# One decoder step: rankings and pairs of the third token tile spread over its u and v rows, element sums gathered 14 rows ahead in pieces of 8, and two final norms moved among the tail's rows

## The chip, the core and the metric

The program runs on one core of a Trainium2 chip. The metric is the device time of one execution in microseconds (us). Four compute engines matter: TensorE (PE in the rows), VectorE (DVE), ScalarE (ACT) and GpSimd (POOL); SyncE (SP) issues loads. All transfers go through the core's 16 DMA engines. Everything is float32.

## What is computed

One layer of a hybrid decoder for 512 prompt tokens and 32 sample tokens: three gated branches (a recurrent block, latent attention, cross-attention) are merged and added to x, then comes PEER, a lookup of experts, and a last RMSNorm. The change touches PEER and what follows it:

```python
q = einsum('td,dhpk->thpk', hb, w_peer_query)              # 8 heads, 2 halves, 128
s = einsum('thpk,hpnk->thpn', q, peer_sub_keys)            # 128 scores per half
s1, i1 = top_k(s[:, :, 0], 16); s2, i2 = top_k(s[:, :, 1], 16)
cand = s1[..., :, None] + s2[..., None, :]                 # 16 x 16 pairs per head
top, sel = top_k(cand, 16); idx = the 16 pairs' expert numbers
w = softmax(top)
act = gelu(einsum('thkd,td->thk', peer_u[idx], hb))
out = einsum('thk,thkd->td', w * act, peer_v[idx])         # 128 rows of 2048 per token
y = rmsnorm(x + out, g_final)
```

## The kernel before

Tokens are cut into tiles of 128: tile 3, tile 4 (the 32 samples), and tiles 0, 1, 2. Each token picks 8 x 16 = 128 experts. One "row" of the kernel is one indirect gather of 128 x 2048 floats, which brings expert number r for each of the tile's 128 tokens: 1,048,576 bytes. `JOBS` is the order of rows: u and v of tile 3, u and v of tile 4 (32 rows each, since the samples are folded four to a partition group), u of tile 2, then v of tiles 2, 0 and 1. GpSimd issues every row (L615) into a ring of five buffers (six in the v rows from tile 2 on). It issues a row only when VectorE has used the row that held the buffer before (`rows_used`). VectorE uses a u row by a multiply with a sum (L2072) and a v row by a multiply-add (L2097 for the samples, L2275 into PSUM for tiles 2, 0, 1).

Tiles 0 and 1 (`DENSE`) have no u rows. In their stead TensorE multiplies their activations with all 16,384 experts (L1217, 128 loads of 1 MiB, the "dense" stage), ScalarE copies each block of 512 columns out (L1566) and stores it to a DRAM tensor `products`. When all are stored, GpSimd gathers the needed sums from it one element per token at a time (L645, the "element gathers", 256 of them), and VectorE turns them into weights a piece of `CHUNK` at a time: `chunk_in` waits for the piece and does the first half of the gelu, ScalarE does the tanh, `chunk_out` the rest. GpSimd holds the element gathers back until v row `HELD` of tile 2, where it waits for the last stored product. From there each v row is followed by one element gather, or by two until it is `AHEAD` rows ahead.

The order on VectorE is written out by hand. `take(n)` uses the next n rows, `upto(r)` uses rows up to a given one. In the stage before the dense one, the "query stage", TensorE makes 16 query blocks (L1196) and scores them; per block u VectorE ranks tile 2's scores (`rank_b`, six instructions, L1987 to L2195) and then takes rows. TensorE may run two blocks ahead of the ranking. `pairs_b(t, h0)` makes the candidate pairs of two heads, ranks them and writes their expert numbers; GpSimd waits for these numbers (`idx_ready`) before rows that need them. `rank_kept` ranks four of the 32 stored score blocks of tiles 0 and 1. The queues on each engine are in order, so whatever waits holds what is written behind it. The final norm of a tile is `square` on ScalarE, `norm_scale` on VectorE, a root on ScalarE, `norm_rows` on VectorE, and a store by SyncE in the order of `FINAL`.

## Time and profile before

| | before |
|---|---|
| median of 3 runs | 4435.69 us (4435.52 to 4441.54) |
| profiled execution, span | 4435.2 us (its own time is not listed apart; the lowest listed run is 0.3 us above the span, the median 0.5 us) |
| PE busy | 3608.9 us (81%) |
| DVE busy | 2800.4 us (63%) |
| ACT busy | 387.1 us (9%) |
| POOL busy | 1465.4 us (33%) |
| moved by DMA | 1409.18 MB, 318 GB/s over the span |

Shares over the whole span mix stages with different limits. The last query block ends before 2785.69 us, the dense stage runs from there to 3660.65 us, and what follows to 4435.2 us is v rows with no TensorE work to speak of (here "the tail"). A megabyte of these rows is 10^6 bytes, so that one gathered row counts 1.0486 MB.

### The profile page before, as it was taken

What the parts mean: (1) busy time and instruction counts of PE and PEld (TensorE: products, weight loads), DVE (VectorE), ACT (ScalarE), POOL (GpSimd) and SP (SyncE); (2) the same over time, 40 slices, a digit from 0 to 9 for tenths busy, and PEclk for the clock granted to TensorE, in tenths of its full rate; (3) what the DMA queues carried; (4) which work ended last, traced back from release to release, by engine and by line L of the source; (5) the groups of instructions that cost most, each with busy time, mean ns of one, the idle gap of its engine ahead of it and who ended that gap; (6) DMA issues with size and microseconds to landing.
All of it is one profiled execution on the core that took longest, in us unless ns stands there. A gap on an engine that the chain in (4) does not pass through costs nothing.

```text
span 4435.2 us, 37982 instructions
## 1 busy us (share of the span) xinstructions
PE 3608.9 (81%) x13874; PEld 2263.2 (51%) x13874; DVE 2800.4 (63%) x3704; ACT 387.1 (9%) x897; POOL 1465.4 (33%) x1217
## 2 busy tenths in 40 slices
PE   9999999998999999999999999999999990000000
PEld 7888856645998575555555456444444440000000
DVE  5233324431000378887887668888885558999998
ACT  1012123321000100000000010000000001000000
POOL 0000100042000035454455444333322226777772
PEclk9999999999999999999999999999999995555555
DMA  4211361158666599999999989999999999999998
GB/s 183 76 68 67 118 222 43 43 185 293 244 240 247 207 390 399 412 418 400 384 406 421 418 358 370 412 405 417 419 401 423 423 423 374 395 409 410 410 410 368
DMA packets 224180, 1409.18 MB, mean 318 GB/s; under 512 B 33312, under 2 KB 44448, under 8 KB 60000
## 3 DMA queue, kind: packets, MB, share of 16 engines
q0 software_dynamic: 135632, 899.39, 50.0%
q1 hardware_dynamic: 75072, 471.89, 27.7%
q10 hardware_dynamic: 13296, 35.52, 2.1%
q8 instruction: 110, 1.80, 0.2%
q14 instruction: 70, 0.57, 0.0%
HBM read 1380.91 MB, written 25.75 MB: 317 GB/s over the span
## 4 chain that ended last, share of the span: by engine, by line
PE 69%; DMA 12%; DVE 6%; POOL 6%; issue 6%; ACT 1%; SPq 0%; DVEq 0%; POOLq 0%; ACTq 0%
PE psum L1217 20%; PE psum L1076 17%; PE psum L670 13%; DMA arena<-in_v,arena 10%; POOL arena L615 4%; PE psum L1196 4%; PE psum L1181 3%; POOL arena L645 2%; DVE arena L2111 2%; DVE psum L2275 2%; PE psum L1144 2%; PE psum L1124 1%; PE psum L743 1%; PE psum L753 1%; PE psum L904 1%
## 5 line engine op out<-in xcount | busy, mean ns | idle before, releaser
L1076 PE MATMUL psum<-arena 128*128 128x160 f32 (+1 forms) x5120 | 1174.1, 393 | 2.6 <-DMA arena<-in_w_merge 1.8
L2275 DVE SCALAR_TENSOR_TENSOR psum<-arena,psum 128x2048 f32<-128x2048 f32 x381 | 897.1, 2355 | 215.4 <-DMA arena<-in_v,arena 207.9
L1076 PEld LDWEIGHTS psum<-arena 128*128 128x128 f32 x5120 | 834.2, 190 | 342.1 <-DMA arena<-in_w_merge 2.0
L615 POOL DMA_INDIRECT arena<-in_v,arena x544 | 638.9, 1174 | 783.3 <-DVE psum L2275 365.0
L1217 PE MATMUL psum<-arena 128*128 128x512 f32 x2048 | 879.2, 592 | 0.6 <-ACT arena L1559 0.6
L615 POOL DMA_INDIRECT arena<-in_u,arena x288 | 462.2, 1605 | 1131.7 <-DVE arena L2028 504.0
L1217 PEld LDWEIGHTS psum<-arena 128*128 128x128 f32 x2048 | 389.1, 190 | 490.1 <-issue 490.1
L670 PE MATMUL psum<-arena 128*128 128x272 f32 x2432 | 565.0, 394 | 8.7 <-DMA arena<-in_w_proj 8.7
L670 PEld LDWEIGHTS psum<-arena 128*128 128x128 f32 x2432 | 461.9, 191 | 108.8 <-issue 14.8
L2072 DVE CUSTOM_DVE_ANT_1 arena<-arena 128x2048 f32<-128x2048 f32 x160 | 361.7, 2289 | 59.6 <-DMA arena<-in_u,arena 58.8
L2111 DVE SCALAR_TENSOR_TENSOR arena<-arena,pages 128x2048 f32<-128x2048 f32 x128 | 300.9, 2351 | 87.6 <-DMA arena<-in_v,arena 83.7
L2072 DVE CUSTOM_DVE_ANT_0 arena<-arena 128x2048 f32<-128x2048 f32 x128 | 288.5, 2289 | 20.1 <-DMA arena<-in_u,arena 18.1
L645 POOL DMA_INDIRECT arena<-products,arena x256 | 247.3, 966 | 94.1 <-issue 79.8
L562 POOL DMA_INDIRECT arena<-in_pool_keys,pages x48 | 45.9, 955 | 434.4 <-PE psum L885 415.3
L1196 PE MATMUL psum<-arena 128*128 128x384 f32 x512 | 167.7, 486 | 1.3 <-ACT arena L1491 1.3
L1181 PE MATMUL psum<-arena 128*128 128x512 f32 x384 | 167.7, 596 | 0.0
L1652 DVE TENSOR_TENSOR arena<-psum,arena 128x544 f32<-128x544 f32 x31 | 22.4, 724 | 219.3 <-PE psum L670 217.6
L550 POOL TENSOR_TENSOR arena<-arena 128x544 f32<-128x544 f32 x16 | 21.7, 1396 | 359.2 <-PE psum L670 359.2
L1471 ACT ACTIVATE arena<-psum 128x160 f32<-128x160 f32 (+1 forms) x96 | 38.1, 397 | 1125.7 <-PE psum L1076 1105.6
L1196 PEld LDWEIGHTS psum<-arena 128*128 128x128 f32 x512 | 96.2, 190 | 65.4 <-ACT arena L1491 1.6
L1181 PEld LDWEIGHTS psum<-arena 128*128 128x128 f32 x384 | 72.8, 192 | 88.1 <-issue 87.9
L1929 DVE SCALAR_TENSOR_TENSOR arena<-arena,psum 128x160 f32<-128x160 f32 (+1 forms) x32 | 14.0, 436 | 164.4 <-PE psum L1076 164.1
(312 smaller groups left out, 2559.4 us busy)
## 6 DMA issues: line engine op xcount, KB each, us to landing
arena<-in_w_merge SPq DMA_DIRECT2D x160, 1024.0 KB, 6.7
arena<-in_u_cols SPq DMA_DIRECT2D x128, 1024.0 KB, 9.5
arena<-in_w_out SPq DMA_DIRECT2D x32, 1024.0 KB, 6.3
arena<-in_w_query SPq DMA_DIRECT2D x32, 1024.0 KB, 6.9
arena<-in_w_proj SPq DMA_DIRECT2D x31, 1024.0 KB, 4.9
products<-arena ACTq DMA_DIRECT2D x32, 512.0 KB, 13.8
arena<-in_pool_keys SPq DMA_DIRECT2D x80, 160.0 KB
arena<-in_v,arena POOLq DMA_INDIRECT x544, 12.0
```

The source lines that it names most:

```text
L562: pool.indirect_dma_start(key_slots[2 * n % KSLOTS][:, j, :], None, A["pool_keys"], bass.IndirectOffsetOnAxis(ap=page_rows[:, pg:pg + 1], ...
L615: pool.indirect_dma_start(row, None, A[table], bass.IndirectOffsetOnAxis(ap=idx[:, r:r + 1], axis=0))\
L645: pool.indirect_dma_start(dense_acts[:, e:e + 1], None, products, bass.IndirectOffsetOnAxis(ap=elem_idx[:, e // P, e % P:e % P + 1], axis=0))\
L670: last = mm(out[:, a, :], w, rhs[:, a * HALF:(a + 1) * HALF], start=start, stop=stop)
L1076: last = mm(out, w[:, (off + k) * P:(off + k + 1) * P], src[:, k0 + k, lo:hi], start=(k == 0), stop=(k == n - 1))
L1144: last = mm(psum[:, 5 + u % 2, 0:A_N], w[:, k * P:(k + 1) * P], hfT_a[:, k, :], start=(k == 0), stop=(k == KD - 1))
L1181: last = mm(psum[:, 3 * (n % 2) + t, :], merged_b[:, 4 * q + k, t * P:(t + 1) * P], w[:, k, :], start=(q == 0 and k == 0), stop=(q == 3 an ...
L1196: last = mm(psum[:, u % 2, 0:B_N], w[:, k * P:(k + 1) * P], hfT_b[:, k, :], start=(k == 0), stop=(k == KD - 1))
L1217: last = mm(psum[:, 4 + DENSE * (b % 2) + t, :], hfT_b[:, k0 + k, t * P:(t + 1) * P], w[:, k, :], start=(k0 + k == 0), stop=(k0 + k == KD ...
L2072: V.tensor_tensor_reduce(row, row, h, 1.0, 0.0, ALU.mult, ALU.add, out).then_inc(s("rows_used"), 1)
L2111: V.scalar_tensor_tensor(lone, row, atmp_3[:, r:r + 1], lone, ALU.mult, ALU.add).then_inc(s("rows_used"), 1)
L2275: V.scalar_tensor_tensor(a, four(row), atmp_b[:, t, r:r + 1], a if r else four(x1_b[:, t, :]), ALU.mult, ALU.add).then_inc(s("rows_used"), 1)
```

## The change

- In the query stage, VectorE takes no rows at u = 0 to 3 and at u = 8, two at u = 9, three at the others (before: three at each but u = 3). The pairs of heads 0 and 1 of tile 2 are made one head at a time, at u = 1 and u = 3; those of heads 2 and 3 at u = 8.
- After it, the first stored ranking comes at u row 36 of tile 2 (before: at the 31st), the groups of four follow at distances of 5 and 6 rows (before 4 or so), the pairs of tile 0 behind u rows 99 to 117, and all four pairs of tile 1 go among the v rows of tile 2 (before: one of them).
- `HELD` goes from 100 to 116, `AHEAD` from 36 to 14, `CHUNK` from 32 to 8; the element gathers count on three semaphores in turn instead of two.
- The final norms of tile 3 and of the samples move from v rows 116 to 123 of tile 2 to v rows 12 to 43 of tile 0. Tile 2's norm now comes first in `FINAL`. The samples' sum uses PSUM banks 0 to 3 once tile 2's norm has read them.
- Three one-use semaphores become one (`lam_ready`).

```diff
-FINAL = (3, 4, 2, 0, 1)
-HELD = 100
-AHEAD = 36
-CHUNK = 32
+FINAL = (2, 3, 4, 0, 1)
+HELD = 116
+AHEAD = 14
+CHUNK = 8
+ELEMS = 3
@@ def idx_count(t, r)
-    return 4 * PAIRS.index(t) + r // 32 + 1
+    split = t < 2 or (t == 2 and r >= 16)
+    return 4 * PAIRS.index(t) + r // 32 + 1 + split
@@ GpSimd
-                    if table == "u" and t != 4 and r % 32 == 0:
+                    if table == "u" and t != 4 and (r % 32 == 0 or (t, r) == (2, 16)):
-                                .then_inc(s(f"elems_landed{e // CHUNK % 2}"), 16)
+                                .then_inc(s(f"elems_landed{e // CHUNK % ELEMS}"), 16)
@@ TensorE
             pe.wait_ge(s("x1_done"), 2)
+            pe.wait_ge(s("y_done"), 1)
             for n in range(4):
-                last = mm(psum[0:SAMP, 4 + n, :], gather4, ...)
+                last = mm(psum[0:SAMP, n, :], gather4, ...)
@@ ScalarE, behind the last product
-            act.wait_ge(s("x1_done"), 1)
-            square("fin", 3, spare, lone)
-            norm_root("fin", 3, 0)
-            act.wait_ge(s("x1_sample"), 1)
-            square("fin", 4, spare[0:SAMP], x1_s[0:SAMP])
-            norm_root("fin", 4, 1)
-            for turn, t, chunks in ((2, 2, (0,)), (3, 0, (1, 2, 3, 4)), (4, 1, (5, 6, 7))):
-                for k in chunks:
-                    gelu_chunk(k)
-                act.wait_ge(s("x1_done"), turn + 1)
-                square("fin", t, four(spare), acc[turn % 2])
-                norm_root("fin", t, turn)
+            per = P // CHUNK
+            gelu_chunks(0, 1)
+            act.wait_ge(s("x1_done"), 3)
+            square("fin", 2, four(spare), acc[0])
+            norm_root("fin", 2, 0)
+            gelu_chunks(1, 2)
+            act.wait_ge(s("x1_done"), 1)
+            square("fin", 3, spare, lone)
+            norm_root("fin", 3, 1)
+            gelu_chunks(2, 4)
+            act.wait_ge(s("x1_sample"), 1)
+            square("fin", 4, spare[0:SAMP], x1_s[0:SAMP])
+            gelu_chunks(4, 5)
+            norm_root("fin", 4, 2)
+            gelu_chunks(5, per + 1)
...
@@ VectorE, pairs of nh heads instead of two
-            def pairs(t, h0, v16, i16, cand, eq, small, rows_between):
+            def pairs(t, h0, v16, i16, cand, eq, small, rows_between, nh=2):
@@ VectorE, query stage, for u in range(16)
-                if u == 3:
-                    pairs_b(2, 0)
-                take(0 if u == 3 else 3)
+                if u in (1, 3):
+                    pairs_b(2, u // 2, 0, 1)
+                if u == 8:
+                    pairs_b(2, 2)
+                take(0 if u < 4 or u == 8 else 2 if u == 9 else 3)
@@ VectorE, u rows of tile 2
-            upto(1)
-            pairs_b(2, 2)
             for n in range(4):
-                upto(7 + 4 * n)
+                upto(36 + 5 * n)
                 rank_kept(4 * n)
-            upto(24)
+            upto(56)
             pairs_b(2, 4)
             for n in range(4):
-                upto((31, 35, 40, 44)[n])
+                upto(63 + 6 * n)
                 rank_kept(16 + 4 * n)
...
+            for n in range(4):
+                upto(99 + 6 * n)
+                pairs_b(0, 2 * n)
+            upto(122)
             share_tops(w_b[:, 2:3, :], tsum_b[:, 2 * PH:3 * PH], 2, s("w_b_ready"))
-            pairs_b(1, 4)
-            upto(P - early - 1)
+            upto(P)
@@ VectorE, v rows
-                        if r == 5:
-                            pairs_b(1, 6, 0)
-                        if r == 10:
+                        if r in (4, 11, 18, 25):
+                            pairs_b(1, 2 * (r // 7), 0)
+                        if r == 32:
                             shift_tops(w_b[:, 0:2, :], tsum_b[:, 0:2 * PH], (0, 1))
...
-                        if r == 116:
-                            norm_scale("fin", 3, 0)
+                    if job == 1:
+                        if r == 12:
+                            norm_scale("fin", 3, 1)
+                        if r == 18:
+                            norm_rows("fin", 3, 1, lone, lone, gain_f, "y_done")
...
+                        if r == 43:
+                            norm_rows("fin", 4, 2, x1_s[0:SAMP], x1_s[0:SAMP], gain_f[0:SAMP], "y_done")
```

The first place is VectorE in the query stage. Before, each ranking of a block (six instructions that begin with MAX) is followed by three v rows of the samples (L2097); here stand the end of one ranking, its rows, and the ranking behind them.

```order
L1993 MAX arena<-arena 128x8
L1995 MAX_INDEX arena<-arena 128x8
L2195 CAST arena<-arena 128x16
L2097 SCALAR_TENSOR_TENSOR arena<-arena,newmask 128x2048 x3
L1987 MAX arena<-psum 128x8
```

After, between the same ranking (its CAST is now L2214) and the next one there is no row; rows stand again only behind u = 4. These are the rankings of u = 2 and u = 3 and the beginning of one head's pairs (L2031):

```order
L2214 CAST arena<-arena 128x16
L2005 MAX arena<-psum 128x8
L2007 MAX_INDEX arena<-arena,psum 128x8
L2009 MATCH_REPLACE arena<-arena,psum 128x128
L2011 MAX arena<-arena 128x8
L2013 MAX_INDEX arena<-arena 128x8
L2214 CAST arena<-arena 128x16
L2031 TENSOR_TENSOR arena<-arena 128x256
```

In all, 47 rows stand in the query stage before (three at 15 of the blocks, two inside the pairs), and 34 now. The other 13 stand behind it, where 26 rows now follow one another before the first stored ranking.

The second place is GpSimd where the element gathers (`products`) begin among the v rows. Before, they begin behind 101 rows:

```order
L615 DMA arena<-in_u,arena 128x2048 x128
L615 DMA arena<-in_v,arena 128x2048 x101
L645 DMA arena<-products,arena 128x1
L615 DMA arena<-in_v,arena 128x2048
L645 DMA arena<-products,arena 128x1
```

After, behind 117 rows, and the double ones are two instead of eight; the second fence is the place where they stand.

```order
L622 DMA arena<-in_u,arena 128x2048 x128
L622 DMA arena<-in_v,arena 128x2048 x117
L652 DMA arena<-products,arena 128x1
L622 DMA arena<-in_v,arena 128x2048
L652 DMA arena<-products,arena 128x1
```

```order
L652 DMA arena<-products,arena 128x1
L622 DMA arena<-in_v,arena 128x2048
L652 DMA arena<-products,arena 128x1 x2
L622 DMA arena<-in_v,arena 128x2048
L652 DMA arena<-products,arena 128x1 x2
L622 DMA arena<-in_v,arena 128x2048
L652 DMA arena<-products,arena 128x1
```

The number of element gathers is 256 in both; the rows that follow the last one are 36 before and 14 now.

The third place is VectorE among the v rows of tile 0 in the changed kernel: rows (L2281), the second half of a piece (L2083, L2084), the norm of tile 3 (L1992), the first half of the next piece (L2078, L2079), and the samples' sum (L2314).

```order
L2083 SCALAR_TENSOR_TENSOR arena<-arena 128x8
L2084 SCALAR_TENSOR_TENSOR arena<-arena 128x8
L2281 SCALAR_TENSOR_TENSOR psum<-arena,psum 128x2048 x3
L1992 SCALAR_TENSOR_TENSOR arena<-arena,vec 128x2048
L2281 SCALAR_TENSOR_TENSOR psum<-arena,psum 128x2048 x3
L2078 SCALAR_TENSOR_TENSOR arena<-arena 128x8
L2079 SCALAR_TENSOR_TENSOR arena<-arena 128x8
L2281 SCALAR_TENSOR_TENSOR psum<-arena,psum 128x2048 x2
L2083 SCALAR_TENSOR_TENSOR arena<-arena 128x8
L2084 SCALAR_TENSOR_TENSOR arena<-arena 128x8
L2281 SCALAR_TENSOR_TENSOR psum<-arena,psum 128x2048 x4
L2314 TENSOR_TENSOR arena<-arena,psum 32x2048
```

Before, 30 rows stand between a piece's second half and the next piece; now six, with pieces of 128x8 where they were 128x32.

## Rows read from the trace of the kernel before

**Rows 1.** The page, part 2: GB/s in 40 slices of 110.9 us.
```profile
GB/s 183 76 68 67 118 222 43 43 185 293 244 240 247 207 390 399 412 418 400 384 406 421 418 358 370 412 405 417 419 401 423 423 423 374 395 409 410 410 410 368
```

**Rows 2.** Windows: start:end length, busy (count) by engine, PEclk, DMA share, GB/s.
```profile
2630.00:2700.00 70.00, 70.00 (x244) 42.99 (x243) 58.93 (x99) 6.28 (x21) 24.85 (x15) 1.00 0.83 315
2803.00:3240.00 437.00, 437.00 (x1020) 193.55 (x1019) 380.19 (x761) 22.10 (x35) 149.41 (x101) 1.00 1.01 415
3240.00:3270.00 30.00, 30.00 (x71) 13.26 (x71) 25.64 (x49) 1.26 (x2) 9.93 (x6) 1.00 0.91 340
3270.00:3660.00 390.00, 390.00 (x911) 172.61 (x910) 234.06 (x134) 18.34 (x30) 89.11 (x96) 1.00 1.01 423
3660.00:3680.00 20.00, 8.48 (x20) 2.67 (x18) 14.09 (x6) 4.55 (x5) 5.45 (x6) 0.81 0.87 348
3680.00:3740.00 60.00, 0.00 (x0) 0.00 (x0) 53.48 (x25) 2.20 (x3) 45.69 (x47) 0.50 1.01 403
3740.00:3800.00 60.00, 0.00 (x0) 0.00 (x0) 49.87 (x30) 6.45 (x8) 46.19 (x46) 0.50 0.91 344
3800.00:4320.00 520.00, 0.00 (x0) 0.00 (x0) 481.49 (x230) 6.11 (x11) 383.59 (x405) 0.50 1.02 410
4320.00:4400.00 80.00, 0.00 (x0) 0.00 (x0) 75.62 (x36) 0.23 (x1) 30.92 (x33) 0.50 1.01 420
```

**Rows 3.** Chain that ended last: start, us, engine, line; end of queries, dense stage.
```profile
2762.24 10.32 PE psum L1196 x32
2773.22 10.32 PE psum L1196 x32
2785.69 874.96 PE psum L1217 x2039
3660.65 12.19 DMA arena<-in_v,arena
```

**Rows 4.** Timeline of DVE in the query stage: start, us, operation [idle before].
```profile
2665.97 0.69 DVE L2012 TENSOR_TENSOR arena<-arena 128x512 f32<-128x512 f32 x1
...
2683.40 0.30 DVE L1987 MAX8 arena<-psum 128x8 f32<-128x128 f32 x1 [0.17 <-DVE arena L2028]
...
2685.91 7.13 DVE L2097 SCALAR_TENSOR_TENSOR arena<-arena,newmask 128x2048 f32<-128x2048 f32 x3
```

**Rows 5.** Groups by shape, DVE, 2803 to 3240: busy, mean ns, idle before.
```profile
L2072 DVE CUSTOM_DVE_ANT_0 arena<-arena 128x2048 f32<-128x2048 f32 x101 | 227.9, 2289 | 18.7 <-DMA arena<-in_u,arena 17.3
```

**Rows 6.** Timeline of POOL where the third tile's u rows end and v rows begin.
```profile
3253.98 1.04 POOL L615 DMA_INDIRECT arena<-in_v,arena  x1 [11.94 <-DVE arena L2072]
```

**Rows 7.** Timeline of POOL behind PE's last matmul.
```profile
3660.65 0.94 POOL L615 DMA_INDIRECT arena<-in_v,arena  x1 [1.55 <-DVE psum L2275]
3674.27 0.95 POOL L645 DMA_INDIRECT arena<-products,arena  x1 [12.69 <-issue]
...
3729.16 3.07 POOL L645 DMA_INDIRECT arena<-products,arena  x1 [0.31 <-issue]
...
3752.91 0.95 POOL L645 DMA_INDIRECT arena<-products,arena  x1 [0.30 <-DVE psum L2275]
3754.16 0.94 POOL L615 DMA_INDIRECT arena<-in_v,arena  x1 [0.30 <-issue]
```

**Rows 8.** Timeline of DVE at the norm of tile 3 and the first piece of element sums.
```profile
3729.06 2.35 DVE L1974 SCALAR_TENSOR_TENSOR arena<-arena,vec 128x2048 f32<-128x2048 f32 x1
...
3758.22 0.19 DVE L2059 SCALAR_TENSOR_TENSOR arena<-arena 128x32 f32<-128x32 f32 x1 [5.53 <-DMA arena<-products,arena]
...
3758.55 4.74 DVE L2275 SCALAR_TENSOR_TENSOR psum<-arena,psum 128x2048 f32<-128x2048 f32 x2
```

**Rows 9.** Groups by shape, 3800 to 4320: busy, mean ns, idle before.
```profile
L2275 DVE SCALAR_TENSOR_TENSOR psum<-arena,psum 128x2048 f32<-128x2048 f32 x202 | 475.7, 2355 | 40.0 <-DMA arena<-in_v,arena 38.0 <-DVE psum L2275 0.4
L615 POOL DMA_INDIRECT arena<-in_v,arena x202 | 192.3, 952 | 71.0 <-issue 64.0 <-DVE psum L2275 7.0
```

**Rows 10.** Window of the fastest 10 us in the dense stage.
```profile
3290.00:3300.00 10.00, 10.00 (x25) 4.46 (x24) 8.79 (x23) 0.00 (x0) 0.00 (x0) 1.00 1.03 428
```

More of the change, by code:

```diff
@@ L1222, in _ @@
             pe.wait_ge(s("x1_done"), 2)
+            pe.wait_ge(s("y_done"), 1)
             for n in range(4):
-                last = mm(psum[0:SAMP, 4 + n, :], gather4, acc_s[:, n * 512:(n + 1) * 512], start=True, stop=True)
+                last = mm(psum[0:SAMP, n, :], gather4, acc_s[:, n * 512:(n + 1) * 512], start=True, stop=True)
             last.then_inc(s("sample_summed"), 1)
@@ L1230, in _ @@
             a_ = nc.scalar.activation
-            own = Count(s("act_step"))
             act.dma_start(vec[:, 0:NVEC], A["vectors"]).then_inc(s("vec_landed"), 16)
@@ L1581, in _, with gelu_chunks @@
             act.wait_ge(s("ffn_rms"), 5)
+            def gelu_chunks(lo, hi):
+                for k in range(lo, hi):
+                    gelu_tanh(4 + k, chunk_of(k))
+            per = P // CHUNK
[4 more added lines that the diff above has]
+            gelu_chunks(1, 2)
             act.wait_ge(s("x1_done"), 1)
             square("fin", 3, spare, lone)
[L1585 removed]
+            norm_root("fin", 3, 1)
+            gelu_chunks(2, 4)
             act.wait_ge(s("x1_sample"), 1)
             square("fin", 4, spare[0:SAMP], x1_s[0:SAMP])
[L1588 to L1597 removed]
+            gelu_chunks(4, 5)
+            norm_root("fin", 4, 2)
+            gelu_chunks(5, per + 1)
+            act.wait_ge(s("x1_done"), 4)
+            square("fin", 0, four(spare), acc[1])
+            norm_root("fin", 0, 3)
+            gelu_chunks(per + 1, 2 * per)
+            act.wait_ge(s("x1_done"), 5)
+            square("fin", 1, four(spare), acc[0])
+            norm_root("fin", 1, 4)
         @block.vector
```

103 lines of the change are left out of this document (43 added, 60 removed).

## The prediction

> **What bounds the kernel now.** I read the slices of the page first, then the chain, then windows cut at the stages, then the timelines of GpSimd and VectorE at the places where those windows sag. The slices show that from slice 14 on the DMA engines move about 400 GB/s nearly without a break, with a ceiling just over 420 [rows 1]. The chain names TensorE until 3660.65 us and v gathers behind it [rows 3]. TensorE's dense stage has its own pace: 874.96 us without a gap. But the end isn't set by it alone. 283 v rows and 256 element gathers are still to be issued when it is over, and each row of 1.0486 MB costs the DMA engines about 2.5 us: 1.0486 MB at 420 GB/s is 2.50 us, the rate of the stretch with rows alone, and at 410 GB/s, with an element gather beside each row, 2.56 us [rows 2]. So I count bytes. Weights, products, rows and outputs are the same in both kernels; the end moves only by what the DMA engines fail to carry. A row used later before 3660 is a row more in the tail, and a sag filled is a row less.
>
> The sags of before, against 423 GB/s in the dense stage (its rate from 3270 to 3660), 420 at its end and 410 in the tail, all from the windows [rows 2]:
> - Query stage, 2630 to 2700: 315 GB/s.
> - Dense stage, 2803 to 3240: 415, so 8 x 437 us = 3.5 MB not carried. VectorE is busy 380 of the 437 us; four stored rankings with four rows between take 4 x 2.51 + 4 x 2.29 = 19.2 us, 4.8 us per row, where the DMA engines would bring one in 4.18 (423 GB/s less 128 MiB of weights and 32 products of 0.52 MB over the stage's 874.96 us leaves 251). Here VectorE was the slower one. (A ranking is 2683.40 to 2685.91 in [rows 4], a u row 2.29 us by [rows 5].)
> - 3240 to 3270: 340, so 83 x 30 = 2.5 MB. GpSimd waits 11.94 us for VectorE, which makes the pairs of tile 1 among the last u rows [rows 6].
> - 3660 to 3800: GpSimd stands 12.69 us at the wait for the last product, then issues two element gathers per row, each 1.25 us [rows 7], until a piece of 32 is complete; VectorE waits 5.53 us for it [rows 8]. That is 72 x 20 + 7 x 60 + 66 x 60 = 5.8 MB, or 14.2 us at 410 GB/s.
>
> **The change, part by part.**
>
> *Rows taken from the query stage.* The stage is paced by TensorE, one block in 10.98 us (2762.24 to 2773.22 in [rows 3]). VectorE takes 13 rows less in it (34 for 47), and GpSimd can't run ahead, since five buffers are all there are. I find nothing that gives VectorE these rows back before 2803 us: from u = 10 on both orders have a ranking of 2.5 us and three rows, 7.13 us, per block [rows 4], inside the 10.98. The pairs at u = 8 (12.7 us, which is 2665.97 to 2683.40 less two rows of 2.36, and two rows) are caught up by u = 12 and hold up no one, TensorE being allowed two blocks. So the dense stage begins when it did, with 13 rows, 13.6 MB, more to carry. Until TensorE ends they can only take the place of other rows, so they are paid in the tail: 13 x 2.50 = **+32.5 us**.
>
> *Rankings and pairs spread.* A group of four rankings now has five rows: (10.0 + 11.5) / 5 = 4.3 us per row, near the DMA engines' 4.18; later six rows, 4.0. The pairs of tile 0 stand six rows apart, (12.7 + 13.7) / 6 = 4.4, a little above. So most of the 3.5 MB comes back. The gap at 3240: no pairs stand there now, but the first v row still needs the buffer of a u row three from the end, so I leave 0.5 MB. All would be 6.0 MB (14.2 us at 423 GB/s), nothing would be 0. I take 4.5 MB: **-10.6 us**. The pairs of tile 1 stand seven rows apart among v rows (12.7 + 7 x 2.355 = 29.2 us, 4.2 per row), level, worth nothing either way. ScalarE now waits longer for `top_shifted` behind product block 21 and may stop TensorE for a few us. TensorE would ask for its weights later, the rows would have the bandwidth in the meantime, and products are wanted later than before (next item). Cost 0; if it were a stop of 30 us or more it would begin to reach the first element gather.
>
> *HELD 116.* At 3660.65 GpSimd issued row 100 of tile 2 [rows 7]. With 13 rows more and some 4 regained it will be near row 91. It reaches row 116 some 25 x 2.5 = 62 us later, long after the last store; the 12.69 us wait goes, and nothing takes its place.
>
> *AHEAD 14, pieces of 8.* Double gathers stand at two rows instead of eight, so GpSimd isn't behind the DMA engines for long. The last element of a piece is issued with row 8k - 7, thus (six buffers) once VectorE has used row 8k - 13, ten rows or 25 us before `chunk_in`; the gather behind 3660.65 took 12.19 us [rows 3]. The 5.53 us wait goes. 24 more pieces cost VectorE 0.33 us each at the first half (3758.22 to 3758.55 in [rows 8]), I take 0.6 for the second: 22 us in all. VectorE stood idle 40.0 us over 202 rows of the tail, which is 51 us over 256 [rows 9]. It is covered, but half of the cover is used.
>
> *Norms in tile 0's rows.* Three `norm_rows` and the samples' sum, 2.35 us each [rows 8], and three `norm_scale` come to some 10 us within 43 rows, with five pieces' 4.6 us. Idle time there is 43 x 0.2 = 8.5 us, so VectorE falls some 6 us back. Six buffers hold about 12 us of DMA work; it is absorbed, with a small sag. Of the tail's 5.8 MB I take back 5.0 (bounds 3.5 and 5.8): **-12 us**.
>
> *Semaphores joined, order of FINAL:* the former are in the first stages, where no wait gets longer; the last tile's norm closes the kernel as before. 0.
>
> A rule speaks against the pieces and the norms. While VectorE ran tile 3's `norm_rows` from 3729.06 us, between two SBUF operands, the gather of 3729.16 took 3.07 us instead of 0.95 [rows 7, 8]. The Trainium skill, "SBUF — State Buffer", section "SBUF: two separate sides", says that VectorE operations with two SBUF inputs and GpSimd shut each other out for the whole instruction. By that rule the 24 added pieces (four such operations each, about 0.19 us) could hold GpSimd for 18 us; by the row of mean durations, 952 ns with pieces of 32 among them, next to nothing. It is priced in the second rival.
>
> **Sum.** +32.5 - 10.6 - 12 = +9.9 us. On the profiled execution's span of 4435.2 that is 4445.1, and the median of the runs lies 0.5 above the span: **4445.5 us**. All sags filled gives +32.5 - 14.2 - 14.2 = +4.1.
>
> **The rivals.**
> 1. *The sags fill entirely.* For it: the spacing is level with the DMA pace, and buffers even out the rest. Against: level is not below. 4435.7 + 4 = 4440 us, no change to be measured.
> 2. *The tail becomes bound by an engine.* VectorE's 6 us aren't absorbed, and GpSimd, at 2 x 1.25 us for a row with its element gather against 2.56 for the DMA engines (0.06 x 256 = 15 us of room), loses 18 us to the pieces. 4445.5 + 6 + 3 = 4455 us. Against: mean gather 952 ns beside such pieces [rows 9].
> 3. *Not slower: the dense stage has room above 423 GB/s.* 10 us at 428 occur [rows 10]. Were 430 the true ceiling and rows merely late, 7 x 857 us = 6 MB more would be carried, another -14 us, and with all sags filled 4435.7 + 4 - 14 = 4426 us. It decides from 427 GB/s on (-8 us and full recovery give 4432). Against: 390 us stand at 423 with VectorE idle for want of rows. The Trainium skill, "DMA: Bandwidth & Descriptors", section "Where 436 GB/s comes from", puts the ceiling at 435; by it, 12 x 857 = 10 MB, or -24 us, and a time near 4415 us. No stretch here comes near it.
> 4. *The spread doesn't fill the dense stage.* If VectorE's bursts, and not its average, made the 415, bursts of pairs are still there: +32.5 - 3 - 12 = 4453 us.
>
> **Chances.** Forecast (4442 to 4450) 0.42; rival 1 (4437 to 4442) 0.25; rival 2 (4451 to 4465) 0.18; rival 3 0.08; rival 4 0.07. Range: leaving out rival 3, the top of rival 2 and a sliver of rival 1 leaves 4437 to 4456. What can be told from no change is 0.2%, 8.9 us: slower means above 4444.6. Six tenths of the forecast, and rivals 2 and 4, give 0.50 slower; most of rival 3 gives 0.07 faster; 0.43 between.
>
> **What the new profile would show.** The query window 2630 to 2700 falls from 315 to some 200 GB/s. The first v gather of tile 2, issued at 3253.98 us before [rows 6], comes near 3290. From 2803 to 3240 the rate is 420 or more, and no 12 us gap lies at the change to v rows. GpSimd issues v row 90 to 93 of tile 2 when TensorE ends, with no wait of 12 us behind it, and the 344 GB/s window is gone. I am wrong if the rows in the dense stage come faster than one in 4.2 us, if the query window doesn't fall, or if the tail's rate with element gathers leaves 408 to 411 for long.

## The result, and the profile after

| | before | changed |
|---|---|---|
| median of 5 runs | 4436.86 us (4435.52 to 4441.54) | 4456.27 us (4453.16 to 4467.37) |
| ratio | | 1.0046, 95% interval [1.0033, 1.0058] |

The kernel became slower by 19.4 us, where the forecast said 9.9 (4445.5). The sign was right, the forecast change was half of the measured one, and the time lies 0.3 us above the range. The same kernel measured again (e6 below) gave 1.0036 [1.0022, 1.0049], 15.8 us. The two, and the spans compared below, put the loss at some 16 to 19 us.

The profiled execution of the changed kernel is the longest of its five: 4467.37 us, span 4465.6. Its query stage begins at 2620.67 us, that of before at 2608.78. This is the stage's first product, before and then after (timeline of PE: start, us, operation, idle before).

```profile
2608.78 16.39 PE L1196 MATMUL psum<-arena 128*128 128x384 f32 x50 [1.34 <-ACT arena L1491]
```

```profile
2620.67 19.80 PE L1203 MATMUL psum<-arena 128*128 128x384 f32 x56 [1.35 <-ACT arena L1498]
```

The order of work up to there is the same in both, and single executions of one kernel differ by this much: e6 is the changed kernel too, and its stage begins at 2607.80. So I compare from the start of the query stage, not from the start of the program. From there to the end before takes 1826.4 us, after 1844.9 (4465.6 - 2620.67), e6 1845.9: 18.5 and 19.5 us more.

Windows cut at the same distances from that start, 194 us (queries), 858 (dense), 140 (where TensorE ends) and 600 (tail). First before, then after; columns as in [rows 2].

```profile
2608.78:2802.78 194.00, 193.37 (x648) 115.88 (x649) 160.32 (x254) 22.50 (x58) 87.68 (x51) 1.00 0.93 367
2802.78:3660.78 858.00, 858.00 (x2000) 379.85 (x1999) 640.66 (x942) 41.71 (x67) 248.80 (x203) 1.00 1.01 416
3660.78:3800.78 140.00, 7.70 (x18) 2.32 (x16) 117.44 (x60) 13.21 (x16) 97.94 (x98) 0.54 0.95 370
3800.78:4400.78 600.00, 0.00 (x0) 0.00 (x0) 556.97 (x266) 6.34 (x12) 413.75 (x437) 0.50 1.02 411
```

```profile
2620.67:2814.67 194.00, 193.37 (x645) 115.98 (x646) 141.85 (x268) 22.50 (x58) 64.60 (x37) 0.99 0.75 290
2814.67:3672.67 858.00, 845.05 (x1966) 373.86 (x1965) 641.14 (x931) 41.56 (x67) 249.48 (x207) 0.99 1.01 419
3672.67:3812.67 140.00, 20.68 (x49) 8.85 (x47) 122.65 (x63) 9.60 (x12) 74.17 (x77) 0.58 1.02 416
3812.67:4412.67 600.00, 5.31 (x8) 1.09 (x8) 569.65 (x355) 17.03 (x41) 437.93 (x460) 0.51 1.02 409
```

Each difference in the last column, times the length of its window, is a number of megabytes. Queries: (290 - 367) x 194 us = -14.9 MB, and GpSimd issues 37 gathers where it issued 51. Dense: +3 x 858 = +2.6 MB (each rounded GB/s is half a unit either way, so the difference is good to 0.9 MB; e6 has +2, 1.7 MB). End of TensorE: +46 x 140 = +6.4. Tail: -2 x 600 = -1.2. Together -7.1 MB; at 0.41 MB per us that is 17 us, against 18.5 measured. The byte count accounts for the time; what was wrong is two of its entries, the query stage's and above all the dense stage's.

What answers to the stages of [rows 2], in the changed kernel:

```profile
2630.00:2700.00 70.00, 70.00 (x242) 42.96 (x241) 37.56 (x99) 6.11 (x19) 10.82 (x6) 1.00 0.44 161
2803.00:3240.00 437.00, 424.05 (x985) 187.48 (x984) 339.86 (x629) 20.76 (x33) 146.54 (x105) 0.98 1.01 417
3240.00:3270.00 30.00, 30.00 (x71) 13.29 (x70) 27.74 (x48) 1.27 (x2) 12.12 (x8) 1.00 1.01 414
3270.00:3660.00 390.00, 390.00 (x910) 172.71 (x909) 275.32 (x269) 18.27 (x30) 95.23 (x95) 1.00 1.01 422
3660.00:3680.00 20.00, 20.00 (x48) 8.85 (x47) 11.78 (x5) 1.27 (x2) 4.36 (x5) 1.00 1.02 423
3680.00:3740.00 60.00, 13.36 (x32) 5.59 (x30) 51.81 (x22) 1.27 (x2) 19.99 (x22) 0.63 1.01 422
3740.00:3800.00 60.00, 0.00 (x0) 0.00 (x0) 55.25 (x28) 3.46 (x4) 43.10 (x44) 0.50 1.02 411
3800.00:4320.00 520.00, 5.31 (x8) 1.09 (x8) 494.74 (x312) 20.86 (x42) 380.56 (x401) 0.51 1.02 410
4320.00:4400.00 80.00, 0.00 (x0) 0.00 (x0) 75.48 (x48) 0.83 (x4) 59.35 (x63) 0.50 1.01 407
```

The query window fell to 161 GB/s, below the 200 I had named: GpSimd issues nothing for 53.73 us, having filled its five buffers.

```profile
2638.82 0.94 POOL L622 DMA_INDIRECT arena<-in_v,arena  x1 [0.30 <-issue]
2693.49 2.39 POOL L622 DMA_INDIRECT arena<-in_v,arena  x1 [53.73 <-DVE arena L2116]
```

The 340 of 3240 to 3270 is 414. In the changed kernel the change from u to v rows lies later, at 3305.93; the 30 us around it, cut as 3240 to 3270 was cut around 3253.98, have 412, so the gap did not merely move:

```profile
3291.93:3321.93 30.00, 30.00 (x71) 13.29 (x70) 20.64 (x23) 1.27 (x2) 13.82 (x10) 1.00 1.01 412
```

The 348 and 344 behind TensorE's end are 423 and 411. But 2803 to 3240 went from 415 to 417 only; 420 was predicted. And the last window has 407 for 420, since the element gathers now run 22 rows longer.

TensorE did stop, at another place than I named. Waits from 2790 to 3670 (engine, line, released by: us in all, times, longest) and the two timelines around it:

```profile
ACT arena L1578 <- DVE arena L2064: 63.8, 1, 63.8
ACT arena L1585 <- DVE arena L2064: 34.3, 1, 34.3
```

```profile
3168.28 0.31 ACT L1578 ACTIVATE arena<-arena 128x128 f32<-128x128 f32 x1 [63.84 <-DVE arena L2064]
```

```profile
3169.31 30.93 PE L1224 MATMUL psum<-arena 128*128 128x512 f32 x67 [12.95 <-ACT arena L1573]
```

ScalarE stands 63.84 us at the exp behind product block 10, because `shift_tops` of tile 2 now comes at u row 92 (before: at the 77th) and VectorE is 13 rows late besides. In its queue behind the exp is the copy of the next product block; TensorE has four PSUM banks for products, two per block, fills them, and stops 12.95 us. Block 21, which the prediction named, waits 34.3 us and stops nobody.

GpSimd at the end of TensorE, to be read against [rows 7]:

```profile
3745.64 0.94 POOL L622 DMA_INDIRECT arena<-in_v,arena  x1 [1.54 <-DVE psum L2281]
3746.88 0.95 POOL L652 DMA_INDIRECT arena<-products,arena  x1 [0.30 <-issue]
```

Row 116 goes out at 3745.64 and its element gather follows without a wait (12.69 us before). TensorE ends near 3687, which is its start at 2799.1 and 874.96 us of work [rows 3] and the stop of 12.95; 22 rows before row 116 one is issued at 3687.31, so it ended at row 94 (90 to 93 predicted, without the stop). The first v gather of tile 2 is issued at 3305.93:

```profile
3305.93 0.94 POOL L622 DMA_INDIRECT arena<-in_v,arena  x1 [7.26 <-DVE arena L2091]
```

3305.93 - 3253.98 [rows 6] is 52.0 us, of which 11.9 are the late start: 40.1 us. Predicted was near 3290, 36 us. The wait ahead of it is still 7.26 us.

### The profile page after: what moved, and what is told of

Read it like the earlier page. It is cut to its first block, busy times and chain, and to the rows that moved or that the text cites. A ratio compares the mean times of both kernels' runs of the same rounds, so it can differ in the third digit from the quotient of the medians.

```text
span 4465.6 us, 38125 instructions
## 1 busy us (share of the span) xinstructions
PE 3620.2 (81%) x13874; PEld 2266.0 (51%) x13874; DVE 2818.9 (63%) x3813; ACT 394.7 (9%) x923; POOL 1449.9 (32%) x1217
## 4 chain that ended last, share of the span: by engine, by line
PE 45%; DMA 23%; DVE 16%; issue 9%; POOL 6%; ACT 1%; SPq 0%; DVEq 0%; POOLq 0%; ACTq 0%
DMA arena<-in_v,arena 15%; PE psum L1083 14%; PE psum L677 13%; DMA arena<-in_u,arena 7%; DVE psum L2281 5%; POOL arena L622 4%; DVE arena L2091 3%; PE psum L1188 3%; PE psum L1203 2%; DVE arena L2130 2%; POOL arena L652 2%; PE psum L1151 2%; PE psum L1131 1%; PE psum L750 1%; PE psum L760 1%
## 5 line engine op out<-in xcount | busy, mean ns | idle before, releaser
L2281 DVE SCALAR_TENSOR_TENSOR psum<-arena,psum 128x2048 f32<-128x2048 f32 x381 | 897.1, 2355 | 146.7 <-DMA arena<-in_v,arena 134.3
L1224 PE MATMUL psum<-arena 128*128 128x512 f32 x2048 | 881.4, 593 | 13.6 <-ACT arena L1573 13.0
L622 POOL DMA_INDIRECT arena<-in_u,arena x288 | 445.7, 1548 | 1154.3 <-DVE arena L2047 505.4
L677 PEld LDWEIGHTS psum<-arena 128*128 128x128 f32 x2432 | 461.5, 191 | 108.9 <-issue 14.9
```

Of the source, the lines that this page charges most:

```text
L622: pool.indirect_dma_start(row, None, A[table], bass.IndirectOffsetOnAxis(ap=idx[:, r:r + 1], axis=0))\
L677: last = mm(out[:, a, :], w, rhs[:, a * HALF:(a + 1) * HALF], start=start, stop=stop)
L1224: last = mm(psum[:, 4 + DENSE * (b % 2) + t, :], hfT_b[:, k0 + k, t * P:(t + 1) * P], w[:, k, :], start=(k0 + k == 0), stop=(k0 + k == KD ...
L2281: V.scalar_tensor_tensor(a, four(row), atmp_b[:, t, r:r + 1], a if r else four(x1_b[:, t, :]), ALU.mult, ALU.add).then_inc(s("rows_used"), 1)
```

## The experiments

Every ratio is to the kernel before, timed beside it. "Back to the end" is the profiled span less the start of the query stage, which takes the chance of the first 2600 us out of the comparison.

| kernel | ratio to before, 95% | us | query / dense / 140 us, GB/s | back to the end, us |
|---|---|---|---|---|
| before | 1 | | 367 / 416 / 370 | 1826.4 |
| changed | 1.0046 [1.0033, 1.0058] | +19.4 | 290 / 419 / 416 | 1844.9 |
| e6, the same again | 1.0036 [1.0022, 1.0049] | +15.8 | 293 / 418 / 415 | 1845.9 |
| e2 query stage only | 1.0080 [1.0065, 1.0095] | +36.7 | 294 / 413 / 407 | 1863.0 |
| e11 dense spread only | 0.9990 [0.9980, 0.9999] | -5.1 | 367 / 418 / 367 | 1824.2 |
| e3 tail only | 0.9972 [0.9961, 0.9983] | -11.7 | 364 / 416 / 413 | 1817.3 |
| e10 changed, 6 rows back | 0.9994 [0.9985, 1.0003] | -0.7 | 328 / 419 / 412 | 1827.9 |
| e4 changed, 10 rows back | 0.9983 [0.9973, 0.9993] | -9.0 | 343 / 420 / 410 | 1820.4 |
| e9 changed, all 13 back | 0.9964 [0.9950, 0.9977] | -16.4 | 364 / 420 / 410 | 1811.0 |
| e12 tail, gap moved | 0.9973 [0.9962, 0.9983] | -12.5 | 368 / 418 / 413 | 1810.7 |
| e13 e9 spaced wider | 0.9954 [0.9940, 0.9968] | -20.4 | 364 / 419 / 411 | 1811.5 |
| e14 changed, spaced wider | 1.0038 [1.0024, 1.0052] | +14.1 | 294 / 420 / 413 | 1842.8 |

### e2_query_only, e3_tail_only and e11_dense_only: the three parts alone

e2 is the kernel before with the rows of the query stage taken as in the changed kernel; e3 has the tail of the changed kernel alone, e11 its spread of rankings and pairs alone (and the exps later, as in e5).

```diff
 e2, VectorE, query stage; and upto(1), pairs_b(2, 2) behind it goes
-                if u == 3:
-                    pairs_b(2, 0)
-                take(0 if u == 3 else 3)
+                if u in (1, 3):
+                    pairs_b(2, u // 2, 0, 1)
+                if u == 8:
+                    pairs_b(2, 2)
+                take(0 if u < 4 or u == 8 else 2 if u == 9 else 3)
 e3: HELD = 116, AHEAD = 14, CHUNK = 8, ELEMS = 3, FINAL and both norms as changed
 e11: the upto(...) lines and the pairs of tile 1 as changed, pairs_b(2, 2) at u row 25,
      exps at blocks 13 and 24
```

> The kernel before with only the query stage of the changed one (no rows at u = 0 to 3 and 8, heads 0 and 1 paired one at a time, heads 2 and 3 at u = 8). Theory: about 14 rows fewer are issued in the stage, 14.9 MB, and all of it is paid in the tail at about 0.42 MB per us, +35 us, less the 12.7 us stand of GpSimd at v row 100, which row 86 at TensorE's end takes away (1.4 MB, 3.5 us): +32, about 4468. Rival: the dense stage has room and takes some of the rows back, +10 to +15 us. A second rival, that the stage's order hardly matters since rows are only later, gives 4437.

> The kernel before with only the tail of the changed one: HELD 116, AHEAD 14, pieces of 8 on three semaphores, tile 3's and the samples' norms among tile 0's rows, tile 2's norm first; query and dense stage, and pairs among v rows, as before. Theory (bytes): the sags behind TensorE's end (348, 403, 344 GB/s) fill, 5 MB of 5.8, which is -12 us: about 4425. Rival: 32 pieces and the norms make VectorE or GpSimd the bound of the tail; then only the wait at row 100 and the wait for the first piece go, -4 us or nothing, 4433 to 4437, and the rate of the tail falls below 408 GB/s.

> The kernel before with the spread of rankings and pairs alone (tail as before, with its doubled element gathers and pieces of 32). Byte theory: 2 to 3 MB more carried by 3660 us, -5 to -7 us. The prediction's own term was 4.5 MB and -10.6 us. Rival: 0, the spread gives nothing without a backlog of rows.

Measured: +36.7 [29, 42], -11.7 [-17, -8] and -5.1 us [-9, 0]. The three sum to +19.9, the whole is +19.4 and +15.8. Each term of the prediction now has its own size: +32.5 was 36.7, -10.6 was 5.1, -12 was 11.7. Windows of e2 show a second loss, which I had not counted:

```profile
2611.80:2805.80 194.00, 193.36 (x648) 115.89 (x649) 142.55 (x269) 22.49 (x58) 65.75 (x38) 1.00 0.75 294
2805.80:3663.80 858.00, 858.00 (x2000) 379.92 (x1999) 623.53 (x924) 41.77 (x67) 234.77 (x199) 1.00 1.00 413
3663.80:3803.80 140.00, 7.71 (x18) 2.32 (x16) 123.83 (x61) 8.47 (x11) 83.34 (x86) 0.54 1.00 407
```

14.2 MB go in the query stage; with the old spacing behind it the dense stage falls from 416 to 413 as well, 2.6 MB. There rankings and pairs are spaced from the stage's start, and with fewer rows used they crowd before the end of the u rows (argued from the order, not tried by itself). So in the company of the changed query stage the spread brings 5 to 6 GB/s (413 to 419 and 418), 4.3 to 5.1 MB, of which 2.6 only repair this; alone it brings 2 GB/s, 1.7 MB.

The tail's part depends on its company too. In e2, with `HELD` still at 100, the wait for the last product has gone from 12.69 to 2.03 us, since row 100 comes later, and the sag of the double gathers has moved behind 3803 us:

```profile
3770.21 2.06 POOL L646 DMA_INDIRECT arena<-products,arena  x1 [2.03 <-issue]
```

```profile
3803.80:3843.80 40.00, 0.00 (x0) 0.00 (x0) 35.14 (x17) 4.74 (x5) 30.55 (x32) 0.50 0.89 336
```

So e2 has 407 for 370 GB/s over the 140 us (5.2 MB) but 405 for 411 over the 600 us behind (3.6 MB less): 14.2 + 2.6 - 1.6 = 15.2 MB in all, 37 us at 0.41 MB per us. From e2 to the changed kernel the tail's windows gain 9 x 140 and 4 x 600, 3.7 MB, where the tail alone gains 4.8. That the three parts sum to the whole is thus in part a balance of two interactions: the spread gives more beside the changed query stage, and the tail gives less.

e3's window where TensorE ends shows where the tail's gain is:

```profile
3658.80:3798.80 140.00, 10.99 (x22) 3.25 (x20) 128.58 (x71) 11.29 (x15) 86.10 (x91) 0.56 1.01 413
```

413 for 370 over 140 us is 6.0 MB; the 600 us behind it have 409 for 411 and lose 1.2 of it, so 4.8 remain (5.0 taken).

### e7_pieces_only and e8_norms_only: the tail cut in two

```diff
 e7: HELD, AHEAD, CHUNK, ELEMS as changed, norms and FINAL as before
 e8: HELD = 100, AHEAD = 36, CHUNK = 32 as before, norms and FINAL as changed
```

> The kernel before with only HELD 116, AHEAD 14, pieces of 8 on three semaphores; the norms stay at v rows 116 to 123 of the third tile. Theory: the wait at row 100 and the double gathers are the cause of the sags behind TensorE's end, so this alone gives most of the -12 us: -9. Rival: the norms, which hold GpSimd (one gather of 3.07 us beside tile 3's), are a good part of the sag from 3740 on; then -5 or less here and as much in the run with the norms alone.

> The kernel before with only the norms moved (tile 2's first, tile 3's and the samples' among tile 0's rows 12 to 43), HELD 100, AHEAD 36 and pieces of 32 as before. Theory: the wait at row 100 and the double gathers stay, so at most -3 us. Rival: -5 or more, if the norms among the last rows of the third tile made the 344 GB/s window.

Measured: e7 4428.86 us against 4439.75, ratio 0.9974 [0.9965, 0.9983], -10.9 us; e8 4438.14, 0.9996 [0.9987, 1.0005], -1.6. The same 140 us, e7 and then e8:

```profile
3658.90:3798.90 140.00, 9.13 (x21) 2.89 (x19) 131.75 (x74) 13.60 (x18) 86.22 (x87) 0.54 1.01 411
```

```profile
3657.00:3797.00 140.00, 11.57 (x22) 3.36 (x20) 112.33 (x55) 6.84 (x9) 95.14 (x99) 0.55 0.94 368
```

The sag is the element gathers' alone; what `HELD`, `AHEAD` and the smaller pieces give of it each was not tried apart. Moving the norms is worth nothing that can be measured.

### e1_exp_block13 and e5_exps_later: is it TensorE's stop?

```diff
 ScalarE, product blocks; e5 has the last two lines as well
-                if b == 10:
+                if b == 13:
                     act.wait_ge(s("top_shifted"), 3)
                     a_(w_b[:, 2, :], w_b[:, 2, :], ACT.Exp)...
-                if b == 21:
+                if b == 24:
```

> The changed kernel with one edit: ScalarE's exp of the third tile's weights is written behind product block 13 instead of 10, so that ScalarE no longer stands before the shift of the tops. Theory (bytes): the 13 us stop of TensorE in the dense stage let the DMA engines fall to 387 GB/s for 60 us (2.0 MB against their rate of 421), and no later place gives that back, so the time falls by 2.0 MB / 0.41 = 5 us, to about 4451 (before + 14.5). Rival (my prediction's own step): TensorE's stop costs nothing, since rows have the bandwidth meanwhile and the products are wanted late; 4456, no change. The profile should show no wait of TensorE for ScalarE in the dense stage.

> The changed kernel with both exps of ScalarE later: behind product blocks 13 and 24 instead of 10 and 21. With only the first moved, ScalarE stood 60.6 us at block 21 for VectorE and TensorE stopped 8.1 us for it, and the time fell by 4 to 5 us at most. Theory (bytes): without either stop the dense stage carries 1.2 to 2 MB more; against the changed kernel as it is, in all -5 to -8 us, about before + 12. Rival: a stop of TensorE leaves its bandwidth to the rows, so nothing moves beyond the run's noise.

Measured: e1 4456.19 against 4440.17, 1.0035 [1.0023, 1.0047]; e5 4459.38 against 4439.75, 1.0044 [1.0030, 1.0058]; the changed kernel beside it (e6) 1.0036 [1.0022, 1.0049]. In e1 TensorE still stops, 8.1 us, now behind block 21; in e5 it stops nowhere. Neither is faster than the changed kernel, and back to the end e1 takes 1844.4 us and e5 1846.1, where the changed kernel takes 1844.9 and 1845.9. The theory that the stop costs time falls, and with it my expectations for e1 and e5. The windows (437 and 391 us, in front of the end of the u rows and behind it) show the exchange, first of e6, then of e5:

```profile
2801.80:3238.80 437.00, 422.44 (x981) 186.76 (x980) 338.51 (x632) 20.77 (x33) 138.03 (x104) 0.98 1.00 415
3268.80:3659.80 391.00, 391.00 (x912) 173.09 (x911) 273.10 (x250) 19.10 (x32) 95.41 (x96) 1.00 1.01 422
```

```profile
2798.90:3235.90 437.00, 437.00 (x1020) 193.44 (x1019) 334.62 (x622) 22.01 (x35) 142.80 (x104) 1.00 1.01 419
3265.90:3656.90 391.00, 391.00 (x913) 173.10 (x912) 273.12 (x259) 18.36 (x30) 95.31 (x94) 1.00 1.01 419
```

Without the stop 1.7 MB more arrive up to 3236 us, and 1.2 MB fewer behind it, where the sag at the change from u to v rows now lies by itself. Why it is deeper there (394 GB/s over the 30 us around the first v gather) than in e6 (418) stays open.

### e6_after_again: the changed kernel once more

> The changed kernel itself, as the measure for the others on the same chip: before + 19 to 21 us, as first measured. The profile, which the first time had a query stage that began 12 us late for reasons ahead of the change, should now begin it near 2608 us and end near 4453 us if the 12 us were chance.

Measured 4455.52 us against 4439.75, +15.8 where 19 to 21 were expected. TensorE stopped 14.6 us here, ScalarE waited 65.4 and 36.2: the waits belong to the kernel, the late start of 11.9 us doesn't.

### e4_rows_back and e10_half_back: the price of a row

```diff
-                take(0 if u < 4 or u == 8 else 2 if u == 9 else 3)
+                take(0 if u in (3, 8) else 3)                                e4, and e1's exp
+                take(0 if u in (2, 3, 8) else 2 if u == 9 else 3)            e10
```

> The changed kernel with ScalarE's exp behind block 13 and with the rows given back in the query stage: three rows at every block but u = 3 and u = 8 (44 in all with the two inside the pairs, for 34; before had 47). Theory (bytes): ten rows more by the end of the stage, 10.5 MB, are worth 25 us in the tail, and the removed stop 5 us: 4456 - 30 = 4426, faster than both kernels. Rival: VectorE can't do pairs, rankings and 44 rows in 176 us, TensorE's query blocks wait for the rankings and the dense stage starts late; then 4435 to 4445, and the query blocks in the chain stand further apart than 11 us.

> The changed kernel with 6 of its missing rows used in the query stage again. Byte theory: 6 x 1.0486 MB at 0.42 MB per us is 15 us less than the changed kernel, so about +3 us against the kernel before. Since all 13 rows gave back 25 us against the changed kernel, proportionality gives -11.5 us, +6 us against before. Rival (a threshold: the rows matter only from some number on, because something else bounds the query stage's end): less than -6 us or more than -20 against the changed kernel.

Measured: e4 4431.17 us against 4440.17; e10 4439.03 against 4439.76. Their query windows:

```profile
2605.50:2799.50 194.00, 193.35 (x645) 115.90 (x646) 163.09 (x287) 22.52 (x58) 81.08 (x47) 0.99 0.87 343
```

```profile
2616.20:2810.20 194.00, 193.37 (x648) 115.82 (x649) 156.86 (x281) 22.44 (x58) 75.93 (x44) 1.00 0.84 328
```

Against the changed kernel e10 moves 38 x 194 = 7.4 MB more in this stage and ends 17.0 us earlier from its start; e4 moves 10.3 MB more and ends 24.5 us earlier: 2.3 and 2.4 us per MB, or 2.4 to 2.5 per row that GpSimd issued. Against e6 (293 GB/s, 1845.9 us) it is 2.6 per MB both times. There is no threshold. e4 and e10 gave back 10 and 6 rows by VectorE's order, and GpSimd issued 10 and 7 more (47, 44 and 37 gathers; e6 has 38).

### e9_best, e15_best_again: the row price again, and a faster kernel

The kernel before with its own query stage, the changed spread (with `pairs_b(2, 2)` behind u row 25), the changed tail, and the exps of e5.

```diff
+            upto(25)
+            pairs_b(2, 2)
             for n in range(4):
                 upto(36 + 5 * n)
                 rank_kept(4 * n)
```

> The kernel before with its query stage untouched, the changed kernel's spread of rankings and pairs behind it, the changed tail, and ScalarE's two exps later (blocks 13 and 24). Byte theory: the tail alone gave -11.7 us, and the changed kernel's dense stage carried 2.6 MB more than before, at 0.42 MB per us 6 us: about -18 us against the kernel before (ratio 0.996). Rival (the 2.6 MB were only there because the query stage had left more rows to carry, and the DMA queue was already fuller): the spread adds nothing, -12 us. A third outcome, worse than the tail alone, would say that the spread itself costs.

> e9_best once more, as the yardstick for e13_spaced on the same chip: -14 to -18 us against the kernel before.

Measured: 4423.36 us against 4439.76, 0.9964 [0.9950, 0.9977], and on another chip 4421.56 against 4439.88, 0.9964 [0.9950, 0.9978]. The spread adds its 5 us to the tail's 11.7. Against e5, which differs from e9 by the query stage and the place of those pairs alone, 1.0044 / 0.9964 makes the query stage's part 35.6 us, 2.7 us per row of VectorE's order. e2 had 36.7.

### e12_gap_moved, e13_spaced, e14_after_spaced: why the spread gave half

Two theories were left. The spacing may be too tight: by the prediction's own working VectorE needs 4.3 and 4.4 us per row against the 4.18 of the DMA engines, and it priced this at nothing. Or bursts as such leave a ring of five buffers empty for a moment, however far apart they stand. e12 takes only the gap at 3240 away; e13 and e14 widen the spacing of e9 and of the changed kernel.

```diff
 e12, on e3: the pairs of tile 1 from the last u rows to v rows
-            pairs_b(1, 4)
-                        if r == 5:
-                            pairs_b(1, 6, 0)
+                        if r in (5, 14):
+                            pairs_b(1, 4 + 2 * (r // 14), 0)
 e13, on e9
-                upto(36 + 5 * n)          rankings, then pairs of tile 0
+                upto(33 + 6 * n)
-                upto(63 + 6 * n)
+                upto(64 + 7 * n)
-                upto(99 + 6 * n)
+            upto(105); pairs_b(0, 0); upto(114); pairs_b(0, 2)
-                        if r in (4, 11, 18, 25):
+                        if r in (4, 12): pairs of tile 0;  in (20, 28, 36, 44): of tile 1
 e14, on e5: 16 + 7 * n, 53 + 7 * n, 99 + 8 * n, v rows 4, 12, 20, 28, 36
```

> The tail alone (-11.7 us) and one edit more: the pairs that VectorE made among the last u rows of tile 2, where GpSimd waited 12 us, go to v rows 5 and 14. Byte theory: the window of 340 GB/s (30 us) rises to 420, 2.4 MB, -5.7 us more, -17 us in all. Rival: the pairs make the same gap at their new place (in the v rows 414 GB/s at most), and only -12 to -13 us come.

> e9_best with its rankings 6 and 7 rows apart (5 and 6), the pairs of tile 0 nine rows apart, two of them moved among the v rows, and the pairs of tile 1 eight rows apart there (7). Theory A (the failed step was the spacing: where VectorE needs 4.3 to 4.4 us per row against the 4.18 of the DMA engines, each burst leaves some bytes behind): e9's dense stage was 3.3 MB short of 423.5 GB/s; 2 to 2.5 MB of it come, 5 to 6 us less than e9, about -21 us against the kernel before. Theory B (the bursts themselves leave a five-buffer ring empty, however far apart they stand): the same time as e9, within 2 us.

> The changed kernel with only the spacing of rankings and pairs changed (7, 7 and 8 rows apart instead of 5, 6 and 6, from u row 16 on instead of 36, one pair of tile 0 among the v rows) and the two exps at blocks 13 and 28. Its query stage is the changed kernel's. Theory A: the 3.5 MB that the changed kernel leaves in the dense stage fall to 1, so -6 us against the changed kernel, +12 against the kernel before (ratio 1.0027). Theory B: +17 to +19, as the changed kernel itself.

Measured: e12 4427.25 us against 4439.76, 0.9973 [0.9962, 0.9983]; e13 4419.52 against 4439.88, 0.9954 [0.9940, 0.9968]; e14 4453.98, 1.0038 [1.0024, 1.0052]. The 30 us of the gap in e3, and the same 30 us in e12:

```profile
3237.80:3267.80 30.00, 30.00 (x72) 13.26 (x71) 26.25 (x50) 1.27 (x2) 10.05 (x6) 1.00 0.90 344
```

```profile
3237.40:3267.40 30.00, 30.00 (x71) 13.30 (x70) 18.61 (x20) 1.27 (x2) 11.02 (x10) 1.00 1.01 406
```

62 x 30 = 1.9 MB came back, 4.5 us' worth, and e12's profile ends 6.6 us nearer to its query stage than e3's (1810.7 for 1817.3). The median shows 0.8 us of it (-12.5 for -11.7), each with an interval of 5 us either way: inconclusive in the time, where -17 was expected. e13 is 2.0 us below e15 on the same chip and ends at 1811.5, e15 at 1810.5: the same. e14 ends at 1842.8, 2 to 3 us nearer than the changed kernel, where the first theory wanted 6, and its ratio can't be told from that of e6. So wider spacing brings nothing in e13 and at most half of what was asked in e14: as the main cause the first theory falls. The dense stage in three windows, of e15 and then of e13:

```profile
2801.00:3238.00 437.00, 437.00 (x1019) 193.42 (x1018) 364.03 (x707) 21.99 (x35) 147.22 (x102) 1.00 1.01 418
3238.00:3268.00 30.00, 30.00 (x71) 13.30 (x70) 17.13 (x14) 1.26 (x2) 9.54 (x9) 1.00 0.99 400
3268.00:3659.00 391.00, 391.00 (x912) 173.09 (x911) 265.92 (x223) 18.34 (x30) 87.36 (x94) 1.00 1.01 423
```

```profile
2800.50:3237.50 437.00, 437.00 (x1019) 193.42 (x1018) 344.53 (x648) 22.01 (x35) 151.66 (x103) 1.00 1.01 418
3237.50:3267.50 30.00, 30.00 (x71) 13.30 (x70) 16.59 (x16) 1.26 (x2) 10.46 (x9) 1.00 0.96 385
3267.50:3658.50 391.00, 391.00 (x912) 173.09 (x911) 287.44 (x283) 18.36 (x30) 87.15 (x93) 1.00 1.01 423
```

VectorE is 20 us less busy in the first window of e13, and the rate there is 418 in both. The 423 behind it is the rate of v rows with six buffers. But the five buffers of the u rows don't forbid it: in the changed kernel 26 u rows follow one another before the first stored ranking, and over those 100 us the rate is 423, while the next 100 us, with rankings, have 421 (423 and 419 at the same places in e5).

```profile
2815.00:2915.00 100.00, 100.00 (x234) 44.27 (x233) 55.84 (x49) 5.06 (x8) 25.25 (x26) 1.00 1.01 423
2920.00:3020.00 100.00, 100.00 (x234) 44.27 (x233) 84.39 (x204) 4.73 (x8) 33.16 (x23) 1.00 1.01 421
```

This speaks for the second theory, the bursts themselves. No run took all bursts away. And where u rows end a sag remains for 30 us (385 to 406 GB/s in e12, e13 and e15), in which GpSimd waits for the buffers of the last u rows.

## Why the prediction was half right

**What bounds the kernel: right.** The end moves by bytes not delivered. In all 17 profiled executions the megabytes of the four windows (711 to 734) and the time back to the end (1863.0 to 1810.5 us) fit one line of 2.4 us per MB, each within 2 us. Part of that is bookkeeping, since all kernels move the same bytes; what it shows is that whatever is late is paid at the DMA engines' rate. Stops of TensorE up to 14.6 us don't show in the time at all.

**Rows taken from the query stage: right mechanism, somewhat too small.** The prediction counted 13 rows, 13.6 MB, +32.5 us. The stage carried 14.2 to 14.9 MB less, and e2 measured +36.7 (the interval, 29 to 42, holds 32.5); e5 against e9 gives 35.6. GpSimd issued 13 fewer in e2 and e6 (38 for 51), as VectorE's order has it, and 14 fewer in the changed kernel's first profile (37), one row at the window's edge. The prediction left out that fewer rows used also crowd the old order behind them: 2.6 MB in e2's dense stage, against 1.6 MB that came back behind TensorE's end. "So the dense stage begins when it did" held, TensorE being busy 193.37 of the 194 us in both.

**Rankings and pairs spread: the step that failed.** "So most of the 3.5 MB comes back", and 2.0 of 2.5 MB at 3240: 4.5 MB, -10.6 us. The gap came back as said (340 to 414 GB/s, 2.2 MB). Of the 3.5 MB at 2803 to 3240 only 0.9 came (415 to 417; e6 has 415; e5, with no stop of TensorE, 419, but then 419 for 423 behind it). The dense stage as a whole has 2.6 MB more, e6 1.7. The term measured 5.1 us alone, with 1.7 MB, so the shortfall is there without the changed query stage too. The mistake was to compare averages: five rows of 4.3 us against 4.18 called level, and a level pace taken for a full ring. Rival 4 had "VectorE's bursts, and not its average", -3 us for this term and 4453 in all; of my cases priced from this step it comes nearest, and I gave it 0.07, though the trace of before had nothing that spoke for the average. That bursts are what holds the rate at 418 is argued from e13, where wider spacing gave nothing, and from the 423 GB/s of the u rows without bursts; no run shows it by itself.

**ScalarE's wait at `top_shifted`: right in price, wrong in place.** Cost 0, with a stop of 30 us or more as the point where it would reach the element gathers: stops of 12.95, 14.6, 8.1 and 0 us end at the same time. It came behind block 10, not 21; the exp there waits for tile 2's `shift_tops`, which comes 15 rows later in the new order and another 13 rows late.

**HELD, AHEAD, pieces of 8: right.** 12.69 and 5.53 us of waiting are gone, -12 predicted, -11.7 [-17, -8] measured with the norms and -10.9 without them (e7), both on the kernel before; behind the changed query stage the windows gain 3.7 MB, some 9 us. Rival 2's 4455 us is the number nearest to the measured one, by chance: its mechanism, an engine-bound tail, is refuted by the groups by shape from 3800 to 4320, which answer to [rows 9]:

```profile
L2281 DVE SCALAR_TENSOR_TENSOR psum<-arena,psum 128x2048 f32<-128x2048 f32 x198 | 466.1, 2354 | 21.4 <-DMA arena<-in_v,arena 15.2
L622 POOL DMA_INDIRECT arena<-in_v,arena x200 | 192.6, 963 | 74.7 <-issue 63.8 <-DVE psum L2281 10.9
L652 POOL DMA_INDIRECT arena<-products,arena x201 | 189.7, 944 | 65.0 <-issue 54.9 <-DVE psum L2281 10.2
```

A gather's issue takes 963 ns for 952, 2.2 us over 200 rows where the rule of the Trainium skill, "SBUF — State Buffer", section "SBUF: two separate sides", allowed 18 us for the added small pieces. VectorE still waits 15.2 us for rows, so it has cover left. The rate is 410 GB/s as before. What I left out is that the element gathers end 22 rows later: 407 for 420 GB/s at 4320 to 4400, 1.0 MB, which the larger gain at TensorE's end (6.4 MB for 5.0) paid.

**Norms in tile 0's rows: right.** e8, -1.6 us within the noise.

**The base.** In every run since, an execution's time is 1.8 us above its span (4467.37 and 4465.6), so the profiled execution of before took some 4437.0; I took 4435.7. That is 1.3 of the 10.8 us missed. By the parts measured alone the query stage adds some 4, the spread 5.5; their interactions blur these two.

**Rival 3 (room above 423 GB/s)** is refuted: no window of 391 us in the dense stage of any kernel rose over 423.

## What to carry to other kernels

Where all stages share one transfer limit, write a ledger of megabytes per stage from one common start, before you look at waits: a stop of an engine that gives its bandwidth to others is free, and a row left out where the DMA engines have slack costs its full price at the end, 2.4 to 2.8 us here. When a stage runs at 98% of its ceiling, don't book its last 2% as gain because two average rates are level; here only the wide gap, 340 GB/s for 30 us, came back. And cut a change into parts in the company of each other too: a sum of parts that agrees can hide two interactions.
